# Gate and up of a feed-forward by Strassen's seven products, their sums and their product on GpSimd

## The reference, cut to what matters

```python
h2 = rmsnorm(x, norm2_g) * (1.0 + scale2) + shift2
ffn = (jax.nn.silu(h2 @ w_ffn_gate) * (h2 @ w_ffn_up)) @ w_ffn_down     # (1024 x 2816), (1024 x 2816), (2816 x 1024)
x = x + gate2 * ffn
```

## Time and profile before

| | |
|---|---|
| device time, median of 3 runs | 1346.58 us (1346.32 to 1347.82) |
| the profiled execution: device time / its span | 1346.31 us / 1344.6 us |
| PE busy | 1298.2 us, 97% |
| DVE / ACT / POOL busy | 639.8 / 431.6 / 179.7 us (48%, 32%, 13%) |
| chain of waits, shares | PE 85%, POOL 6%, DVE 3%, ACT 3% |
| granted clock, mean | 0.994 |
| HBM over the span | 91 GB/s |

### The profile page before, as it was taken

How to read it: one execution, slowest core, us unless ns; L and a number is a source line. 1 busy time by engine, 2 the same in 40 slices (tenths; PEclk the granted TensorE clock), 3 DMA queues, 4 the chain that set the end, 5 groups by cost and what they waited for, 6 DMA issues and landing times.

```text
span 1344.6 us, 19844 instructions
## 1 busy us (share of the span) xinstructions
PE 1298.2 (97%) x7974; PEld 1190.9 (89%) x7974; DVE 639.8 (48%) x1043; ACT 431.6 (32%) x668; POOL 179.7 (13%) x189
## 2 busy tenths in 40 slices
PE   5999999999999999998999899999999999999997
PEld 2698887799999999986888898899998999889996
DVE  4553213477656543472998644553234222343236
ACT  5352313444211122125777322332121222212224
POOL 1011001301011111112999200000000000000000
PEclk9999999999999999998999999999999999999999
DMA  9533121144444334452000224122213222222211
GB/s 312 188 110 117 63 95 47 53 146 138 138 145 156 110 94 129 129 170 74 1 1 1 95 95 156 63 64 69 87 63 94 63 79 77 66 91 63 78 48 78
DMA packets 87378, 129.37 MB, mean 96 GB/s; under 512 B 3529, under 2 KB 64450, under 8 KB 87186
## 3 DMA queue, kind: packets, MB, share of 16 engines
q1 hardware_dynamic: 76880, 95.17, 21.9%
q0 software_dynamic: 9104, 32.20, 7.8%
q10 hardware_dynamic: 1330, 1.10, 0.3%
HBM read 117.43 MB, written 4.73 MB: 91 GB/s over the span
## 4 chain that ended last, share of the span: by engine, by line
PE 85%; POOL 6%; DVE 3%; ACT 3%; issue 1%; DMA 1%; SPq 0%; ACTq 0%; DVEq 0%
PE psum L389 51%; PE psum L426 25%; POOL probs L840 3%; POOL probs L846 3%; PE psum L876 1%; PE psum L375 1%; DMA ada_a<-in_w_ada 1%; PE psum L562 1%; PE psum L490 1%; PE psum L984 1%; PE psum L982 1%; PE psum L983 0%; ACT probs L1381 0%; PE psum L969 0%; ACT w_hi L353 0%
## 5 line engine op out<-in xcount | busy, mean ns | idle before, releaser
L358 DVE TENSOR_TENSOR w_lo<-w_raw,w_hi 128x2048 fp32r<-128x2048 f32 x77 | 176.4, 2291 | 348.1 <-ACT w_hi L353 345.5
L389 PE MATMUL psum<-h_hi,w_lo 128*128 128x320 f32 x1312 | 300.4, 310 | 0.8 <-ACT y_nat L1324 0.8
L389 PE MATMUL psum<-h_hi,w_hi 128*128 128x320 f32 x1312 | 299.1, 309 | 0.0
L389 PE MATMUL psum<-h_lo,w_hi 128*128 128x320 f32 x1312 | 298.9, 309 | 0.0
L389 PEld LDWEIGHTS psum<-h_hi,w_lo 128*128 128x128 f32 x1312 | 219.0, 188 | 1.9 <-issue 1.7
L389 PEld LDWEIGHTS psum<-h_hi,w_hi 128*128 128x128 f32 x1312 | 219.3, 188 | 0.0
L389 PEld LDWEIGHTS psum<-h_lo,w_hi 128*128 128x128 f32 x1312 | 219.2, 188 | 0.0
L353 ACT ACTIVATE w_hi<-w_raw 128x2048 fp32r<-128x2048 f32 x77 | 146.9, 1908 | 216.9 <-PE psum L426 158.9
L426 PE MATMUL psum<-w_lo,h_hi 128*128 128x512 f32 x240 | 93.7, 390 | 0.4 <-ACT mod L1273 0.4
L426 PE MATMUL psum<-w_hi,h_hi 128*128 128x512 f32 x240 | 93.4, 389 | 0.0
L426 PE MATMUL psum<-w_hi,h_lo 128*128 128x512 f32 x240 | 93.4, 389 | 0.0
(11 more groups left out here) (260 smaller groups left out, 1895.0 us busy)
## 6 DMA issues: line engine op xcount, KB each, us to landing
w_raw<-in_w_in SPq DMA_DIRECT2D x32, 1024.0 KB, 5.4
ada_b<-in_w_ada POOLq DMA_DIRECT2D x32, 512.0 KB, 3.9
w_raw<-in_w_ffn_gate SPq DMA_DIRECT2D x11, 1024.0 KB, 5.2
w_raw<-in_w_ffn_up SPq DMA_DIRECT2D x11, 1024.0 KB, 5.3
ada_a<-in_w_ada SPq DMA_DIRECT2D x8, 1024.0 KB, 14.1
w_raw<-in_w_ffn_down SPq DMA_DIRECT2D x8, 1024.0 KB, 5.1
w_raw<-in_w_ret_out SPq DMA_DIRECT2D x4, 1024.0 KB, 5.0
swapped<-qk_d POOLq DMA_DIRECT2D x32, 128.0 KB, 2.5
```

The costliest lines, as they stand in the source:

```text
L358: dve.tensor_tensor(w_lo[s][:, :, :], w_raw[s][:, :, :], w_hi[s][:, :, :].bitcast(F32), ALU.subtract).then_inc(w_lo_done, 1)
L389: last = pe.matmul(bank(4 * par + 2 * j + h, HALF), w[:, k, cs], x[:, k, h * HALF:(h + 1) * HALF], start=(k == 0 and n == 0), stop=(k == K ...
```

## The change

The first gate and up units stay as they are (a phase `up_first`); the other 20 units are formed by Strassen's method in Winograd's variant. A unit's 1024 x 256 weights are taken as 2x2 blocks of 512 x 128 (B11, B12 above B21, B22; `low_k`, `high_k` are the halves of k), the tokens as 2x2 blocks of 512 k x 320. Seven block products of 4 k x 3 matmuls, 84 in place of 96, take the place of eight. TensorE forms them in the order B11, B21, T1, B22, T2, T4, T3, where

T1 = B12 - B11, T2 = B22 - T1, T3 = B22 - B12, T4 = B21 - T2.

The products go into banks x, y, z, v, x, y, x of the unit's four banks. So T2 waits until ScalarE has copied the first result from bank x (`copy_first`), T4 until VectorE has read y, and T3 until VectorE has read x a second time. These are the names used below:

- **S1 to S4**: GpSimd's sums of weights of a unit in `weight_sums`, 128x512 each: T1; T3 (in place of B12); T2; T4 (in place of B11).
- **high and low of a product**: ScalarE's and VectorE's splits of its 128x512 weights (`act_seven`, `dve_seven`). Seven slots replace the two slots `w_hi`/`w_lo`; a slot is filled for the next unit once this unit's product of that name is formed.
- **R1 to R4**: VectorE's reads of a unit, each 128x320 with one operand in PSUM: R1 = first + y; R2 adds x to `partial` (it is what T3 waits for); R3 and R4 make the second tile's first half.
- **F1 to F3**: the reads after T3 (F1 adds x, F2 and F3 complete tile 1 and tile 0).
- **M1, M2**: GpSimd's 128x640 multiplications of `hid_f` by `silu_g`, both operands in SBUF, after F2 and F3 of an up unit (before: VectorE, one operand in PSUM). The Silu reads and writes SBUF now.
- **Token sums**: four sums of 128x1280 on GpSimd, once, each split high (ScalarE) and low (VectorE). T1's product waits for the first, B22's for all four.

The modulated tokens stay whole in `hf2`; some tiles move to other addresses, and `final_norm_g` is loaded after the first unit of `down2`.

```diff
+        def pe_seven(pe, third, i, par):
...
+            banks = [bank(4 * par + b, HALF) for b in (0, 1, 2, 3, 0, 1, 0)]
+            for p in range(SEVEN):
...
+                if n == 0 and p == T1:
+                    pe.wait_ge(x_sum_l, 1)
+                if n == 0 and p == B22:
+                    pe.wait_ge(x_sum_l, 4)
+                if p == T2:
+                    pe.wait_ge(seven_copy, n + 1)
+                if p == T4:
+                    pe.wait_ge(seven_read, 5 * n + 1)
+                if p == T3:
+                    pe.wait_ge(seven_read, 5 * n + 2)
...
+                for k in range(KH):
+                    for m, (w, x) in enumerate(((seven_lo, x_hi), (seven_hi, x_lo), (seven_hi, x_hi))):
+                        last = pe.matmul(banks[p], w[:, p, k, :], x[:, k, :], start=(k == 0 and m == 0),
+                                         stop=(k == KH - 1 and m == 2))
...
+            def weight_sums(third, i, par):
...
+                pool.wait_ge(w_landed[par], (unit - par) * 8 + 16)
+                if n:
+                    pool.wait_ge(seven_l, (SEVEN - 1) * (n - 1) + T1 + 1)
+                pool.tensor_tensor(t_sum[0][:, :, :], b12, b11, ALU.subtract).then_inc(seven_T, 1)
+                pool.wait_ge(seven_T, 4 * n + T1_DONE)
+                pool.tensor_tensor(b12, b22, b12, ALU.subtract).then_inc(seven_T, 1)
+                if n:
+                    pool.wait_ge(seven_l, (SEVEN - 1) * (n - 1) + T2 + 1)
...
+                pool.tensor_tensor(t_sum[1][:, :, :], b22, t_sum[0][:, :, :], ALU.subtract).then_inc(seven_T, 1)
+                pool.wait_ge(seven_T, 4 * n + T2_DONE)
+                pool.wait_ge(seven_l, (SEVEN - 1) * n + B11 + 1)
+                pool.tensor_tensor(b11, b21, t_sum[1][:, :, :], ALU.subtract).then_inc(seven_T, 1)
+            def hidden(third, i, par):
+                pool.wait_ge(silu_done, seven_index(third, i, par) + 1)
+                for j in range(2):
+                    pool.wait_ge(freed["dve"], freed_after(f"up{third}", i, 1, 1 - j))
+                    pool.tensor_tensor(hid_f[:, 1 - j, :], hid_f[:, 1 - j, :], silu_g[:, 1 - j, :], ALU.mult).then_inc(hid_m, 1)
...
+                for n, unit in enumerate(units):
+                    if n + 1 < len(units):
+                        weight_sums(*units[n + 1])
+                    if unit[2]:
+                        hidden(*unit)
...
+            def seven_units(third):
...
+                for n, unit in enumerate(units):
+                    following = units[n + 1] if n + 1 < len(units) else None
+                    if following:
+                        act_seven(act, *following, B11)
+                    if previous:
+                        finish_unit(*previous)
+                    copy_first(*unit)
+                    if following:
+                        act_seven(act, *following, B21)
+                        act_seven(act, *following, T1)
+                        for p in (B22, T2, T4, T3):
+                            act_seven(act, *following, p)
```

More of the change, by code:

```diff
@@ L108 @@
 SPLIT = len(EARLY) * P
+HID_TILES = (8, 8, 6)
+HID_BASE = (0, 8, 16)
+KH = KT // 2
+SEVEN = 7
+B11, B21, T1, B22, T2, T4, T3 = range(SEVEN)
+T1_DONE, T3_DONE, T2_DONE, T4_DONE = 1, 2, 3, 4
 SETUP_ACT, SETUP_DVE = 14, 8
@@ L133, in ready, with seven_index, first_tile @@
     return i * 4 + (2 * FIRST[name] + 2 * par + j + 1 + AHEAD)
+def seven_index(third, i, par):
+    return sum(COUNT[f"up{n}"] for n in range(third)) + 2 * i + par
+def first_tile(third, i):
+    return 2 * i + (2 if third == 0 else 0)
 def is_long(n):
@@ L1423, in _, with prefill @@
                 if k == 4:
-                    act_split(act, unit_of("up0", 0, 0) + 1, 1)
+                    act_split(act, unit_of("up_first", 0, 0) + 1, 1)
             for k in range(KT):
                 norm2_high(act, k, 1)
-            def up(third):
-                name = f"up{third}"
-                def evacuate(i, par):
-                    for j in range(2):
[L1433 to L1442, removed]
+            def prefill(third, lows, after):
+                for p in lows:
+                    act_seven(act, third, 0, 0, p, after)
@@ new lines, in finish_unit @@
+            def finish_unit(third, i, par):
+                if third == 0 and i < 0:
+                    for j in range(2):
+                        high_of_hidden(j, j)
+                elif par == 0:
+                    for j in (1, 0):
+                        act.wait_ge(freed["dve"], freed_after(f"up{third}", i, 0, 1 - j))
+                        act.activation(silu_g[:, j, :], silu_g[:, j, :], ACT.Silu).then_inc(silu_done, 1)
+                else:
+                    for j in range(2):
+                        high_of_hidden(HID_BASE[third] + first_tile(third, i) + j, j)
@@ L1444, in _, with before_next, prefill_next @@
+            def before_next(third):
+                def prefill_next():
+                    prefill(third + 1, (B11, B21, T1, B22), ready(f"down{third}", 1, 0, 1))
+                    prefill(third + 1, (T2, T4, T3), ready(f"down{third}", 1, 1, 1))
+                return prefill_next
             set_table(ACT.Silu)
             for third in range(3):
-                (dense if third else dense_after_split)(f"up{third}", up(third))
+                if third == 0:
+                    first_pair()
+                seven_units(third)
```

285 lines of the change are left out of this document (232 added, 53 removed).

## The result

| | before | after |
|---|---|---|
| device time, median of 4 runs | 1346.69 us (1346.32 to 1347.82) | 1362.53 us (1361.15 to 1363.73) |
| profiled execution / its span | 1346.31 / 1344.6 us | 1361.15 / 1359.5 us |
| granted clock, mean | 0.994 | 0.985 |

The ratio is 1.0116, with a 95% interval of 1.0098 to 1.0133: slower by 1.2%, 16 us. The forecast was 1356, slower. One of its rivals, the falling clock, came on top of the forecast's own mechanism.

A forecast was written before the change was run, and what follows sets the result against it. PE (matmul time) was taken to bound the kernel: -34.7 for removed matmuls, +27.3 for seven gate-unit stalls, +4.2 and +12.8 for first gate units gave +9.6, 1356 us; range 1325 to 1374, the forecast's own 1350 to 1363.

The forecast's parts named there:

- the falling clock: Rival: PE's stalls in gate units behind a pair also drop the clock to half; about 1373 us, chance 0.18.
- the forecast's own mechanism: DVE and POOL instructions with two SBUF operands exclude each other, so R2 comes late in gate units; 1356 us, chance 0.42.
- the turns in DVE's favour: Rival: in a gate unit S4 comes behind the low of T1, stall 2.7 us; 1343.5 us, chance 0.15.
- Nothing excludes: Rival: exclusion of DVE and POOL weaker or turns fall well, gate-unit stall 0.3 us; 1319 us, chance 0.20.
- The stall: PE's wait for R2 before T3's product in a gate unit behind a pair: 3.9 us, seven times, 27.3 us.
- just met: In a gate unit behind a pair, `copy_first` ends at 6.8 us, T2 wants it at 6.95: no wait.
- my price of 10 to 24 us: Addition if the clock falls: 1.5 to 3.4 us lost behind each of seven gate-unit stalls.
- my two cases: Lengths of a half-clock stretch behind a PE gap, 2.9 and 6.8 us, each losing half of itself.
- The objection: Argument against a falling clock: the earlier stall at 629 had little work before it, here PE is full.
- PE's busy time falls by some 35 us: Sign that the forecast is right: over the kernel PE's busy time falls this much, its idle time grows by more.
- The first unit of `up0`: First gate unit, waiting for token sums and what queues behind them: 12.8 us lost, 5.4 without exclusion.
- The first units of `up1` and `up2`: Gate units with no pair before them, R2 ending 12.5 us after the start, wanted at 10.42: 2 x 2.1 = 4.2 us.

The follow-up runs named there:

- e1: Kernel after without GpSimd's four sums of weights per unit (memsets of one column instead): 1324.65 us, ratio to the kernel before 0.9841.
- e3: Kernel after without the multiplications M1 and M2 (memsets of one column instead), sums kept: 1329.52 us, ratio to the kernel before 0.9875.
- e5: Kernel after with the multiplications M1 and M2 on VectorE behind F3, nothing left out: 1329.41 us, ratio to the kernel before 0.9879.
- e6: Kernel after with VectorE's lows of B21 and T1 and both `hid_lo` moved behind R4: 1328.41 us, ratio to the kernel before 0.9870.
- e4: Kernel after plus 20 matmuls of 320 columns before PE's wait for R2 in seven gate units: 1351.12 us, ratio to the kernel before 1.0042.
- e7: Kernel after with the four token sums on VectorE before its first lows: 1354.47 us, ratio to the kernel before 1.0064.

## Why the prediction was right, and where its terms were off

**The mechanism.** The forecast rested on one chain in the gate unit behind a pair: M2 late, `hid_hi` and `copy_first` behind it, R1, blocked `hid_lo` and low of T1, R2. Each step stands in the trace: R1 ended at 7.9 us after the unit's start (forecast 7.3), S4 began at 11.5 (11.9), the low of T1 ended 13.6 (13.8), R2 14.0 (14.2), and T3's product started at 14.2 (14.3). The turns around M2 fell otherwise than written: the low of T4 ran first, M1 behind it and the low of T3 ahead of M2, so that M2 ended at 5.6 in place of 4.9; that is why R1 was late, and the later steps made it up. Four experiments show the chain as cause: taking away POOL's reads (e1), its M1 and M2 (e3, e5) or what stands ahead of R2 (e6) each ends the gap or leaves 1.1 us of it at most, and returns 33 to 38 us. That DVE's work is too much is refuted by e5, that the longer lows cost by themselves by e3. The up units had no wait for R2, as forecast.

**The rival of the turns in DVE's favour** failed where the prediction placed it: S4 started at 1091.06, in the time of B21's low, and T1's low stood behind it. **Nothing excludes** failed with lows of 1352 ns in the mean.

**The stall was mis-sized**: 3.9 forecast, 3.1 measured for R2. R2 came on time, but T3's product would have been due at 11.1, not at 10.42. Of these 0.7 us, 0.14 are the rate: I took 152 matmuls in 22 us as 0.1447, but such a count includes matmuls that are cut by the window's ends; starts in the timeline are 0.1467 apart. The rest is the copy, which I had called just met and which cost 0.45 (M2's delay again), with 0.07 to restart. With the copy a gate unit lost 3.67 where I had 3.9, 1.6 us less over seven. The rate also moves the saving from 34.7 to 35.2.

**The clock was the step left out of the sum.** I gave it 0.18 as a rival that excludes the forecast, and it is an addition to it: 10.6 us behind the seven stalls, and 10.6 again in the pairs of e4. That is at the low end of my price of 10 to 24 us, since a slow stretch was 3.4 us long, near the shorter of my two cases, and loses 0.45 of itself, not half. The objection, that PE is full up to the gap, was no protection. The sign "PE's busy time falls by some 35 us" failed with it: busy time fell by 18.6, as matmuls at half clock are busy time too.

From my sum to the trace: 9.6 + 10.6 for the clock - 2.4 for the waits in the seven units + 0.8 for the restarts - 2.6 for the first unit - 1.5 for the two others - 0.5 for the rate + 1.0 at the start of `down` = 15.0. That 1356 came within 7 us, and that 1362.5 still lies in the forecast's own 1350 to 1363, is partly luck: terms sized too high made up for half of the one left out.

**The first unit of `up0`** cost 10.2, not 12.8: the four waits were 1.2, 4.4, 0.9 and 1.6 in the view (1.4, 4.5, 1.2 and 1.75 from start to start) in place of 3.0, 4.9, 2.3 and 2.4, whose sum is 12.6 and was rounded up. There was 1.0 of clock in it, which the forecast had not. The first of the token sums:

```profile
888.68 2.97 POOL L987 TENSOR_TENSOR s_sum<-hf 128x1280 f32<-128x1280 f32 x1 [76.89 <-DVE h_lo L737]
```

2.97, inside the 2.5 to 3.2 of the prediction; the fourth took 2.97 too, the two between them 3.33 and 3.41, above it. The first starts 15.3 us ahead of the unit, where I had 14, and the fourth ends 2.6 ahead, where I had 1. **The first units of `up1` and `up2`** cost 1.35 each, 2.1 forecast.

**Not settled.** Why the clock fell behind every gap after and behind three of seven in e7. Whether the turns of DVE and GpSimd fall the same way in other orders of work was not tried.

## What to carry to other kernels

An engine that frees PSUM should read it before it does work in SBUF that another engine can block; a busy share of 58% says nothing on whether one read is late. Work moved to GpSimd to relieve VectorE can lengthen VectorE's own instructions if both read SBUF, and it puts everything that waits for the moved work behind GpSimd's queue: follow that chain to the first thing that the bounding engine needs. A gap of some 3 us of a full TensorE can have a second price behind it, the clock (1.5 us here, behind ten gaps of fourteen in after and e7 together); add it to the sum rather than beside it. And read a wait from start to start of the matmuls: the list of waits gives 0.16 us less for each.

## What the runs showed of the hardware

- DVE's 128x512 with two SBUF operands took 0.68 us alone. Beside a GpSimd instruction that reads SBUF it grew with that one's length: up to 1.79 beside a sum of 128x512 (1.27 alone), up to 2.07 beside M1 and M2 (1.56 alone), and 3.46 beside a token sum of 128x1280; the source view after (ns min/median/max):

```profile
L694 DVE TENSOR_TENSOR seven_lo<-w_raw,seven_hi x100: 676/683/3458, 891.5 to 1298.8; 128x512 fp32r<-128x512 f32 x100
L694 DVE TENSOR_TENSOR seven_lo<-t_sum,seven_hi x40: 677/1618/1792, 903.4 to 1295.3; 128x512 fp32r<-128x512 f32 x40
```

- R2 and F1, one operand in PSUM, stayed at 473 to 489 ns beside the same work.
- A GpSimd memset of 128x512 took 0.53 us, and the lows of T1 and T2 beside it stayed at 686 ns in the mean.
- F32R matmuls of 320 columns started 0.147 us apart at clock 1.00 and 0.267 at 0.50. The clock fell after gaps of 2.9 us with PE full on both sides, but not after each, for 3.4 us at a time; 20 matmuls in the gap kept it at 1.00.
